# The rwkv stage's weights: rounded on ScalarE and rested on VectorE instead of on GpSimd

## The reference, cut to what matters

```python
    fa = token_shift(fa.astype(jnp.float32), mu)
    r, k, v, w_lo, a_lo, g_lo = _split(fa, ...)
    log_decay = -RWKV_DECAY_SCALE * jax.nn.sigmoid(w0 + jnp.tanh(w_lo) @ w_up)
    a = jax.nn.sigmoid(a0 + a_lo @ a_up)
    g = jax.nn.sigmoid(g_lo) @ g_up
    kk = heads(k * k_k)
    kk = kk / jnp.maximum(jnp.sqrt(jnp.sum(kk * kk, axis=-1, keepdims=True)), 1e-12)
    k = k * (1.0 + (a - 1.0) * k_a)
    ...
    def step(s, inp):
        r_t, w_t, k_t, v_t, kk_t, a_t = inp
        sa = jnp.einsum('bhvk,bhk->bhv', s, -kk_t)
        s = (s * w_t[:, :, None, :] + sa[..., None] * (kk_t * a_t)[:, :, None, :]
             + v_t[..., None] * k_t[:, :, None, :])
        return s, jnp.einsum('bhvk,bhk->bhv', s, r_t)
    ...
    y = head_group_norm(y, ...)
    y = y + jnp.sum(r * k * r_k, axis=-1, keepdims=True) * v
    return y.reshape(bsz, t, MIX_WIDTH) * g
```

## Time and profile before

| | |
|---|---|
| median of 3 runs | 4214.64 us (4213.33 to 4217.25) |
| the profiled execution | 4206.03 us, its span 4204.2 us |
| TensorE busy | 3933.3 us, 94% of the span |
| VectorE busy | 1998.1 us, 48% |
| ScalarE busy | 1333.8 us, 32% |
| GpSimd busy | 1147.1 us, 27% |
| mean granted TensorE clock | 0.971 of full speed |

### The profile page before, as it was taken

How to read it: one execution, slowest core, us unless ns; L and a number is a source line. 1 busy time by engine, 2 the same in 40 slices (tenths; PEclk the granted TensorE clock), 3 DMA queues, 4 the chain that set the end, 5 groups by cost and what they waited for, 6 DMA issues and landing times. The chain is left out here.

```text
span 4204.2 us, 45737 instructions
## 1 busy us (share of the span) xinstructions
PE 3933.3 (94%) x18490; PEld 3217.4 (77%) x18490; DVE 1998.1 (48%) x2960; ACT 1333.8 (32%) x2121; POOL 1147.1 (27%) x590
## 2 busy tenths in 40 slices
PE   9998889999899978888989999999998999898998
PEld 7886768887788757777777777888887888676887
DVE  3334763334533365554444556674225362544663
ACT  2223443323322232222333323433322332444332
POOL 0000215552000011111545554454442444231000
PEclk9999999999999989999999999999999999999999
DMA  4332102222233320000212223223331222111222
GB/s 145 98 94 82 36 21 85 81 81 81 82 96 96 97 73 26 26 16 23 71 60 76 76 82 99 95 96 99 96 107 60 96 96 96 55 46 36 94 96 85
DMA packets 92130, 320.98 MB, mean 76 GB/s; under 512 B 10128, under 2 KB 11152, under 8 KB 91664
## 3 DMA queue, kind: packets, MB, share of 16 engines
q1 hardware_dynamic: 91920, 318.06, 23.8%
HBM read 313.82 MB, written 4.19 MB: 76 GB/s over the span
## 5 line engine op out<-in xcount | busy, mean ns | idle before, releaser
L297 POOL TENSOR_TENSOR w_lo<-w_raw,w_hi 128x1024 fp32r<-128x1024 f32 (+2 forms) x386 | 932.0, 2415 | 605.7 <-ACT w_hi L291 586.3
L316 POOL CAST w_hi<-w_raw 128x1024 fp32r<-128x1024 f32 (+1 forms) x200 | 215.6, 1078 | 2091.9 <-issue 1109.4
L329 PE MATMUL s_acc<-xn_hi,w_hi 128*128 128x512 f32 x1824 | 718.6, 394 | 42.3 <-DVE xn_lo L1387 15.8
L329 PE MATMUL s_acc<-xn_hi,w_lo 128*128 128x512 f32 x1824 | 713.9, 391 | 0.0
L329 PE MATMUL s_acc<-xn_lo,w_hi 128*128 128x512 f32 x1824 | 713.8, 391 | 0.0
L291 ACT ACTIVATE w_hi<-w_raw 128x1024 fp32r<-128x1024 f32 (+2 forms) x404 | 416.2, 1031 | 614.7 <-PE s_acc L329 505.0
L329 PEld LDWEIGHTS s_acc<-xn_hi,w_hi 128*128 128x128 f32 x1824 | 345.1, 189 | 124.5 <-DVE xn_lo L1387 18.1
L297 DVE TENSOR_TENSOR w_lo<-w_raw,w_hi 128x1024 fp32r<-128x1024 f32 (+1 forms) x218 | 262.5, 1204 | 356.9 <-ACT w_hi L291 356.1
L329 PEld LDWEIGHTS s_acc<-xn_lo,w_hi 128*128 128x128 f32 x1824 | 345.5, 189 | 72.6 <-issue 1.2
L329 PEld LDWEIGHTS s_acc<-xn_hi,w_lo 128*128 128x128 f32 x1824 | 344.8, 189 | 72.3
L329 PE MATMUL s_acc<-hidden_hi,w_hi 128*128 128x512 f32 x784 | 305.0, 389 | 0.0
(11 more groups left out here) (638 smaller groups left out, 6916.3 us busy)
## 6 DMA issues: line engine op xcount, KB each, us to landing
w_raw<-in_f_up SPq DMA_DIRECT2D x132, 512.0 KB, 3.7
w_raw<-in_mg_w SPq DMA_DIRECT2D x64, 512.0 KB, 3.7
w_raw<-in_g_up SPq DMA_DIRECT2D x64, 512.0 KB, 3.4
w_raw<-in_f_down SPq DMA_DIRECT2D x48, 512.0 KB, 3.5
w_raw<-in_hg_w SPq DMA_DIRECT2D x32, 512.0 KB, 3.9
w_raw<-in_g_down SPq DMA_DIRECT2D x32, 512.0 KB, 3.4
w_raw<-in_fox_w SPq DMA_DIRECT2D x24, 512.0 KB, 3.6
w_raw<-in_f_down SPq DMA_DIRECT2D x24, 384.0 KB, 3.2
```

Source lines behind the costliest of these rows:

```text
L297: eng.tensor_tensor(lo, raw, value, ALU.subtract).then_inc(self.parted, 1)
L316: pool.tensor_copy(hi, raw).then_inc(self.rounded, 1)
L329: last = pe.matmul(out, w[:, slot, tile_cols(k)], v[:, k0 + k, :], start=start and k == 0 and n == 0, stop=stop and k == kt - 1 and n == 2)
```

## The change

GpSimd's block of the stage is removed. ScalarE rounds and VectorE rests the same 17 pieces at places written out by hand: piece 2 at the start, then per round the pieces 5p+3 to 5p+7. `round_first` and `rest_first` walk over three pieces and skip those that are not this stage's, here the first two. In round 3 only 5p+3 = 18 is left.

```diff
@@ -882,10 +882,6 @@
                     ev.done(pe.matmul(b[5][:, :], c.tab("head_ones"), tmp[:, :], start=True, stop=True), "varied")
                 each_round(4, body)
 
-            @block.gpsimd
-            def _(pool):
-                ring.parts(pool)
-
             @block.scalar
             def _(act):
                 q = InOrder(act, achain)
@@ -893,6 +889,8 @@
                 act.activation(lora[0:64, 1, :], lora[0:64, 1, :], ACT.Tanh).then_inc(pre, 1)
                 act.activation(lora[:, 2, :], lora[:, 2, :], ACT.Sigmoid).then_inc(pre, 1)
                 act.wait_ge(zeroed, 1)
+                ring.round_first(act)
+
                 def gate(p, m):
                     act.wait_ge(ring.used, beside[p, m] + 1)
                     act.activation(part_out[:, bass.ds(2 * p + m, 1), :].rearrange("p o t -> p (o t)"), b[1 + m][:, :],
@@ -918,7 +916,10 @@
                     q(act.activation(tmp[:, :], tmp[:, :], ACT.Ln))
                     ev.done(act.activation(tmp[:, :], tmp[:, :], ACT.Exp, scale=-0.5), "rooted")
                     gate(p, 0)
+                    ring.round(act, beside[p, 0] + 3)
                     gate(p, 1)
+                    if not last_round:
+                        ring.round(act, beside[p, 0] + 4)
                     ev.wait(act, "turned", p)
                     for dst, n in ((bt, 1), (kt, 2)):
                         for half in range(2):
@@ -935,11 +936,14 @@
                             ev.done(act.activation(tnv[:, :, :], bank(6), ACT.Copy), "nv_here")
                         if i in fetch and not last_round:
                             ahead.move(act, p + 1, fetch[i])
+                        if i in (1, 3) and not last_round:
+                            ring.round(act, beside[p, 0] + (5 if i == 1 else 6))
                     ev.wait(act, "ta_made", p)
                     q.free(act.activation(ta[:, :, :], bank(0), ACT.Copy, scale=-1.0))
                     ev.done(act.activation(tnv[:, :, :], bank(3), ACT.Copy, scale=-1.0), "ta_here")
                     if not last_round:
                         ahead.move(act, p + 1, 2)
+                        ring.round(act, beside[p, 0] + 7)
                     ev.wait(act, "mixed", p)
                     ev.done(act.activation(kn[heads[1], :], b[2][heads[1], :], ACT.Copy), "gathered1")
                     ev.wait(act, "centred", p)
@@ -966,6 +970,7 @@
                 q(dve.memset(pad[:, :, 0:1], 0.0))
                 q(dve.memset(bt[:, :, :, :], 0.0))
                 dve.memset(kt[:, :, :, :], 0.0).then_inc(zeroed, 1)
+                ring.rest_first(dve)
 
                 def wide(name_):
                     return c.tab(name_).rearrange("p (o t) -> p o t", o=1).broadcast_to([P, TT, P])
@@ -1033,6 +1038,8 @@
                                 ev.done(dve.tensor_tensor(level[:, h, :, :], mt[:, h, :, :], wide(f"level{i + 2}"), ALU.mult), f"level{h}")
                         if i < 3:
                             side(2 * i)
+                        if i == 0 or not last_round and i in (1, 2, 4):
+                            ring.rest(dve, beside[p, 0] + (3, 4, 5, None, 6)[i])
                         for h in range(2):
                             ev.wait(dve, f"tp{h}", p, i)
                             ev.wait(dve, f"updated{h}", p, i)
@@ -1067,6 +1074,8 @@
                     ev.done(dve.tensor_copy(kn[heads[0], :], b[1][heads[0], :]), "gathered0")
                     ev.wait(dve, "meaned", p)
                     ev.done(dve.scalar_tensor_tensor(kn[:, :], b[4][:, :], -1.0 / 64, kn[:, :], ALU.mult, ALU.add), "centred")
+                    if not last_round:
+                        ring.rest(dve, beside[p, 0] + 7)
                     ev.wait(dve, "croot", p)
                     ev.done(dve.tensor_tensor(kn[:, :], kn[:, :], g[:, :], ALU.mult), "scaled")
                     ev.wait(dve, "affine", p)
```

## The result

The changed kernel takes **4181.89 us** (median of 4 runs, 4181.28 to 4183.17) where the kernel before took 4214.44 beside it (4 runs, 4213.33 to 4217.25): a ratio of 0.9922, with a 95% interval of 0.9905 to 0.9939. The forecast was 4186.6, with a range of 4179 to 4200.

What follows compares the result with a forecast made beforehand. TensorE, busy 94% of the span, was taken as the bound, but waiting at round heads for VectorE, slowed by GpSimd. Gains of 23.9 (heads) + 4 (clock) = 28 us off the 4214.6 median gave 4186.6, range 4179 to 4200.

Steps and rivals of the forecast that it cites:

- The contention: In each round's head, GpSimd's overlapping weight work slows VectorE; without it the head is busy 11.3 us.
- The heads, 23.9 us: TensorE's gaps ahead of L778 shrink as VectorE's heads speed up: 6.6 + 7.4 + 7.4 + 2.5 us over four rounds.
- The clock, 4 us: Behind the heads of rounds 0 to 2, TensorE holds 2.4 GHz: 4 us gained over the stage, bounds 0 and 6.
- Rival A: Heads are freed but the clock gives nothing, or later switching points fall worse: 4190.7 us, to 4198; chance 0.27.
- The moved work, cost 0: 17 Copies on ScalarE and 17 remainders on VectorE fit into their waits for TensorE in the stage: cost 0.
- Rival D: New work on VectorE and ScalarE is exposed in each step: 38 us against 28 gained, 4225 us; chance 0.04.
- Rival B: VectorE's remainder in step 0, ahead of L1040, is exposed: 4.8 us less gain, 4191.5 us; chance 0.1.
- The median: Base of the forecast: the whole program's median of 4214.6 us, with the profiled execution 8.6 us below it.
- the 28 us: Forecast gain of the rwkv stage: 23.9 us from the heads plus 4 from the clock, moved work costing 0.

Runs made afterwards that it cites:

- the pair of reads and writes: Changed kernel plus useless GpSimd work beside each head: four subtractions of constant tables, 4209.73 us; ten memsets in their place, 4180.40 us.
- the GpSimd version: Kernel before, GpSimd keeping casts and remainders but holding three pieces a round until VectorE has made the first level products, behind the head: 4179.54 us, ratio 0.9924.
- the fills: Changed kernel plus unread TensorE products of constant tables, three in each round's tail and three in round 3's head: 4175.64 us, ratio 0.992.
- fills and the later GpSimd work: Kernel before with GpSimd's pieces held until behind the head, plus the unread TensorE products in the idle gaps: 4176.80 us, ratio 0.9917.

## Why the prediction was right, point by point

**The contention.** Right, and to the size. The head was forecast at 11.3 us busy and is 11.38 in all rounds. The changed kernel, with GpSimd's remainders or reads put back beside the head, shows the same lengthening at the same kinds of instructions, and the kernel that only moves GpSimd's work in time has the gain. What a trace alone had suggested (a slow instruction wherever GpSimd is busy) the pair of reads and writes bore out. The Trainium skill (SBUF — State Buffer, Who interferes with whom) states it as a rule: a VectorE instruction with two inputs in SBUF contends with a GpSimd instruction that reads SBUF, not with one that only writes it, and the one that comes second is blocked until the other ends. The runs agree: 2.88 us for a 0.69 us operation that started 0.31 us behind a remainder of 2.65, and 0.69 beside memsets.

**The heads, 23.9 us.** Measured: 22.0. Rounds 0 and 1 fit (6.48 for 6.6, 7.41 for 7.4), with L961 of the start in it. Two terms came out smaller. In round 2 the gain is 6.36 and not 7.4, since VectorE had to wait 1.62 us for L770, and in round 3 it is 1.77 and not 2.5, with a wait of 0.96 where the working allowed 0.3. Behind VectorE's two lines stands TensorE's L770 of round 3 in the kernel with three remainders in step 0:

```profile
1750.04 0.69 DVE L995 TENSOR_SCALAR rw_tmp<-rw_b 128x512 f32<-128x512 f32 x1 [1.62 <-PE rw_b L770]
...
1853.19 0.69 DVE L995 TENSOR_SCALAR rw_tmp<-rw_b 128x512 f32<-128x512 f32 x1 [0.96 <-PE rw_b L770]
```
```profile
1855.49 1.13 PE L770 MATMUL rw_b<-rw_tmp,table 128*128 128x512 f32 x2 [2.65 <-ACT rw_tmp L909]
```

Both are the clock's doing. In round 2 L770 was late because the tail before it had run at half clock; where that tail is at full clock, as in the GpSimd version, the wait is 0.58 us and the head 12.28 instead of 13.33. In round 3 TensorE waits 2.65 us for ScalarE's square ahead of L770, and the two products then take 2.01 us at half clock. In the kernel of the last line they stand behind the same 2.65 us, but take 1.13, and VectorE doesn't wait at all: its head lasts 11.78 us instead of 12.67, so the gain is 2.65. ScalarE's square is no later than before: it ends 2.66 us behind the head's first instruction in both kernels. With the clock up, the four heads give 6.48 + 7.41 + 7.40 + 2.65 = 23.94 us, each from the trace in which it stays up. So the sum of the heads was right to 0.1 us, and the 1.9 us that are missing belong to the clock's term.

**The clock, 4 us.** Behind the heads and in the tails the gain is 3.36 + 1.24 = 4.6; less the 1.9 that the clock took back in the heads, the term measures 2.7. That is within its bounds of 0 and 6, but its make-up is not what was said. Behind three of the heads 2.4 GHz holds as forecast, and in rounds 0 and 1 it gives 1.4 us each. But the drop to 1.2 GHz did not only go: one came in another place. Full speed brings TensorE earlier to its wait ahead of step 0's first product, which grew from 0.44 to 1.36 us, and in round 2 the clock fell there. TensorE's timeline before (round 1) and after (rounds 1 and 2):

```profile
1676.02 2.02 PE L811 MATMUL rw_b<-rw_tri,rw_level 128*128 128x128 f32 x16 [0.44 <-DVE rw_tri L1017]
```
```profile
1660.29 2.02 PE L811 MATMUL rw_b<-rw_tri,rw_level 128*128 128x128 f32 x16 [1.36 <-DVE rw_tri L1022]
...
1765.42 3.30 PE L811 MATMUL rw_b<-rw_tri,rw_level 128*128 128x128 f32 x16 [1.36 <-DVE rw_tri L1022]
```

And the tails at half clock were those of rounds 2 and 3 before the change and is that of round 1 after it: +1.83, +0.95 and -1.54 in the table. Rival A had this in it ("later switching points fall worse"). Nothing in the working said that the tails would come out in favour of the change; that part of the sum is luck. Rounds were forecast at 102.5 and are 101.20, 105.13 and 103.15: a clean one is 101.2, a drop in step 0 costs 1.6 (102.75 against 101.16 above), one in the tail some 2.5 with the late L770 behind it, and one behind L841 some 1.4. The last is seen in round 1 in VectorE's wait ahead of its first mask of the growth products (L847), after the change and in the GpSimd version without a drop there:

```profile
1716.13 0.56 DVE L1053 TENSOR_TENSOR rw_mt<-rw_b,table 128x384 f32<-128x384 f32 x1 [8.57 <-PE rw_b L847]
```
```profile
1716.96 0.56 DVE L1053 TENSOR_TENSOR rw_mt<-rw_b,table 128x384 f32<-128x384 f32 x1 [7.17 <-PE rw_b L847]
```

The warning of the Trainium skill (TensorE: Matmul & The Clock Gate, What's actually happening) that where the clock switches is not to be fitted from a count of slow products fits this: with the same wait of 1.36 us the clock fell in round 2 of the changed kernel, in none with the fills, and in rounds 0 to 2 with fills and the later GpSimd work. Between traces of one kernel it differs as well: rounds 0 and 1 of the kernel before took 110.04 and 111.30 us in one trace and 111.48 and 112.71 in the other. The two traces of the changed kernel agree to 0.05 us a round.

**The moved work, cost 0.** Right. ScalarE's wait behind its Copy is 2.50 us; before it stood at 13.64, most of which was the late head and no slack. Rival D, 38 us of exposed work, found nothing. **Rival B** was sized wrong although its verdict came out: it was to decide from 1.29 us on, the idle time ahead of L1040. Doubling the remainder cost nothing; the third cost 1.2 to 1.3 us a round. The 1.29 us was the idle time ahead of one wait of a pair, and between the pair and the next mask there was more.

**The median.** The difference of two profiled executions was set off from the median of 3 runs. That was the right base only roughly: later runs of the kernel before have medians of 4210 to 4211, and against these the changed kernel's 4180.67 is 30 us less, against 26.6 and 29.5 us (439.62 - 410.09) that the pairs of stages show. The gain of the medians in the first comparison, 32.5 us, is 5.9 more than its stage gained. The rest of the program does not explain it: in both pairs of traces it takes 2 to 3 us longer after the change. The four runs of the kernel before in that comparison came out 3 to 4 us above its later medians. So part of the distance between the forecast and the measured time lies in that base and not in the sum, and the 28 us are to be held against the stage's 26.6 and 29.5.

**Open.** Whether the GpSimd version that stays out of the head, or the fills, beat the change: 4179.54, 4176.80 and 4175.64 against 4180.67 and 4181.89, with intervals that overlap. And what decides at which of several like gaps the clock falls, and so whether the added products keep it up or only happened to meet rounds in which it stays up.

## What to carry to other kernels

Before moving work off GpSimd, ask which of VectorE's instructions it lies beside: elementwise work on GpSimd that reads SBUF cost VectorE here, per meeting, about what was left of GpSimd's instruction (2.1 to 2.2 us beside remainders, 0.7 beside casts), and a wait that holds it back until VectorE has slack gives the same gain without loading two other engines. Price a freed engine by what it waits for next, for every round by itself: the same head waited 0, 0.58, 1.62 and 0.96 us for the same product, the last two because TensorE's clock was down. Before calling a longer wait a new limit, look whether the products behind it ran at half clock. Idle time ahead of one wait is a lower bound of the slack; doubling the work in that place measures it.

## What the runs showed of the hardware

- A GpSimd memset left two-input operations alone, but stretched the one-input ones that read SBUF: the TENSOR_SCALAR of 0.43 us took 0.92 beside it, the one of 0.48 took 0.79. The Trainium skill (SBUF — State Buffer, Who interferes with whom) says of copy, cast and tensor_scalar that they can contend with GpSimd in their two-port modes. That L999 is in such a mode is suggested by its 0.43 us against 0.69 for the other operations of this size, and not shown.
- VectorE held GpSimd up little: beside the slow masks a cast took 1.50 us instead of 1.04, a remainder 2.70 instead of 2.35.
- TensorE's clock fell behind the same waits in some rounds and not in others: with 0.78 and 1.45 us in the group norm it fell in round 1 of the changed kernel and not in its rounds 0 and 2; with 1.36 us ahead of step 0's first product it fell in round 2 and not in rounds 0 and 1. With products of no use in the group norm's waits it fell in none of six tails (rounds 0 to 2 of two kernels), which is no proof, since it fell in one of six without them in the two kernels that they were added to.
